# Expert rows past 128: gathered as quarter rows, turned by two 128x128 transposes, their results turned four chunks at a time

## The reference, cut to what matters

```
def moe(h, w_router, b_router, w_gate_up, b_gate_up, w_down, b_down):
    ...
    def expert_block(args):
        xb, e = args
        gu = xb @ w_gate_up[e] + b_gate_up[e]
        gate, up = gu[:, :D_EXPERT], gu[:, D_EXPERT:]
        gate = jnp.minimum(gate, SWIGLU_LIMIT)
        up = jnp.clip(up, -SWIGLU_LIMIT, SWIGLU_LIMIT)
        act = (up + 1.0) * gate * jax.nn.sigmoid(SWIGLU_ALPHA * gate)
        return act @ w_down[e] + b_down[e]
    ...
    y = y * gate_buf[:, None].astype(y.dtype)
    out = jnp.zeros((T + 1, D), y.dtype).at[tok_buf].add(y)[:T]
```

## Time and profile before

| | |
|---|---|
| median of 3 runs | 2743.37 us (2742.76 to 2745.33) |
| the profiled execution: its time | 2737.53 us |
| the profiled execution: span from first to last instruction | 2735.9 us |
| TensorE matmul busy | 2543.6 us, 93% of the span |
| VectorE, ScalarE, GpSimd busy | 850.0, 465.2, 274.2 us |
| mean granted clock of TensorE | 0.974 of full speed |
| experts stage, first to last transposed result | about 994 to 2551 us |

### The profile page before, as it was taken

The page is one execution under the profiler, slowest core; times in us unless marked ns, Lnnn a source line. Parts: engine busy times, 40 slices in busy tenths (PEclk is TensorE's granted clock), DMA queues, the critical chain, the costliest instruction groups (busy, mean ns, idle before and its releaser), DMA issues. The chain is left out here.

```text
span 2735.9 us, 46887 instructions
## 1 busy us (share of the span) xinstructions
PE 2543.6 (93%) x16462; PEld 2051.9 (75%) x16462; DVE 850.0 (31%) x2328; ACT 465.2 (17%) x1072; POOL 274.2 (10%) x421
## 2 busy tenths in 40 slices
PE   5897888999997949999999999999999999999599
PEld 3444665444444449999999999999999999999444
DVE  3425664000012342222222223232333333333353
ACT  3313442000000101111111111111111111111132
POOL 1420000000012210000000000000000000000220
PEclk9999999999998969999999999999999999999799
DMA  4000003011016467888888889899999999997441
GB/s 129 8 19 1 1 0 107 24 46 46 23 40 183 90 226 249 270 259 265 279 272 275 278 271 291 288 290 295 294 315 297 312 300 312 300 312 224 161 161 71
DMA packets 463940, 518.75 MB, mean 190 GB/s; under 512 B 16481, under 2 KB 440049, under 8 KB 463890
## 3 DMA queue, kind: packets, MB, share of 16 engines
q1 hardware_dynamic: 430898, 445.57, 52.4%
q0 software_dynamic: 14368, 38.95, 4.4%
q10 hardware_dynamic: 18624, 33.56, 3.6%
HBM read 484.33 MB, written 33.70 MB: 189 GB/s over the span
## 5 line engine op out<-in xcount | busy, mean ns | idle before, releaser
L1433 PE MATMUL bank<-arena_a,arena_w 128*128 128x128 f32 (+4 forms) x8192 | 977.4, 281 | 2.9 <-DVE bank L1525 2.9
L1433 PEld LDWEIGHTS bank<-arena_a,arena_w 128*128 128x128 f32 x8192 | 971.0, 191 | 3.2 <-issue 3.2
L1451 PE MATMUL bank<-arena_a,arena_w 128*128 128x128 f32 (+4 forms) x4096 | 517.0, 282 | 6.7 <-issue 6.7
L1451 PEld LDWEIGHTS bank<-arena_a,arena_w 128*128 128x128 f32 x4096 | 497.1, 191 | 12.9 <-issue 12.9
L1544 DVE TENSOR_SCALAR arena_m<-bank,arena_m 128x160 f32<-128x160 f32 x256 | 98.3, 384 | 631.1 <-PE bank L1433 631.1
L941 PE MATMUL bank<-arena_h,arena_w 128*128 128x512 f32 x512 | 224.4, 596 | 8.6 <-DMA arena_w<-in_w_pool_out_dram 8.6
L1555 DVE TENSOR_SCALAR arena_m<-bank,arena_m 128x160 f32<-128x160 f32 x256 | 98.3, 384 | 394.7 <-PE bank L1451 389.6
L941 PEld LDWEIGHTS bank<-arena_h,arena_w 128*128 128x128 f32 x512 | 98.0, 192 | 132.0 <-issue 123.2
L1496 ACT ACTIVATE arena_m<-arena_m 128x160 f32<-128x160 f32 x256 | 84.1, 336 | 662.1 <-DVE arena_m L1544 660.9
L1347 POOL DMA_DIRECT2D arena_m<-slot_tokens x33 | 19.4, 589 | 1227.7 <-issue 1225.2
L1502 ACT ACTIVATE arena_a<-bank 128x512 f32<-128x512 f32 x64 | 38.2, 597 | 612.1 <-PE bank L1465 612.1
(11 more groups left out here) (277 smaller groups left out, 2029.7 us busy)
## 6 DMA issues: line engine op xcount, KB each, us to landing
arena_w<-in_w_gate_up_dram SPq DMA_DIRECT2D x248, 1024.0 KB, 6.7
arena_w<-in_w_down_dram SPq DMA_DIRECT2D x124, 1024.0 KB, 6.6
expert_rows<-arena_a ACTq DMA_DIRECT2D x32, 512.0 KB, 2.8
arena_a<-in_x_dram SPq DMA_DIRECT2D x16, 512.0 KB, 4.2
arena_w<-in_w_in_dram SPq DMA_DIRECT2D x16, 512.0 KB, 5.2
arena_w<-in_w_gate_up_dram ACTq DMA_DIRECT2D x8, 1024.0 KB, 14.9
arena_w<-in_w_o_dram SPq DMA_DIRECT2D x1, 4096.0 KB, 16.0
x_rows<-arena_a SPq DMA_DIRECT2D x8, 512.0 KB, 6.7
```

The costliest lines, as they stand in the source:

```text
L1433: m = pe.matmul(GU[f % 3][:, to:to + width], w[c][:, k, at:at + P], xT[:, k, 0:width], start=(k == 0), stop=(k == K - 1), skip_group_check ...
L1451: m = pe.matmul(DN[d % 2][:, 0:width], wd[c][:, k, at:at + P], actT[:, k, 0:width], start=(k == 0), stop=(k == KF - 1))
```

## The change

**Gather.** The 32 rest rows are gathered as 128 quarter rows of 256 channels: row number r and quarter q together sit in partition 32q + r. GpSimd reads the 32 row numbers four times, into four partition groups, computes 4 x number + q in one instruction (with `quarter`, a column of 0, 1, 2, 3 that VectorE fills in the route stage) and gathers 128 pieces of 1 KB into `xq`. **Turning in.** Two 128x128 transposes of `xq` into `DN[0]` (now `x_rest`) replace the eight small ones; the eight main chunks go to `TX` and `DN[1]` (`x_bank`), four to a bank, and `GU[2]` is no longer used. ScalarE empties `TX` in one copy; VectorE empties `x_rest` in one strided copy and `DN[1]` in another. `down`'s first two steps now wait for VectorE's copies. **Turning back.** VectorE's bias add writes main and rest columns apart (`yT`, `yR`, all eight chunks kept), and the rest columns of four chunks are turned by one 128x128 transpose, behind chunks 3 and 7. ScalarE empties both halves of `YB` in one copy and stores them by two DMAs. **Start.** The zeroing of the banks is gone; `yR` and `yT` are zeroed in SBUF.

```diff
+                        for q in range(QUARTERS):
+                            dve.memset(quarter[q * REST:(q + 1) * REST, :], float(q)).then_inc(sem("quarter"), 1)
...
-        xg2 = view(arena_a, D, D)[0:REST, :]
+        QUARTERS = P // REST
+        QW = D // QUARTERS
+        xq = view(arena_a, D, QW)
...
-            pool.dma_start(idx_b, list_dram[bass.ds(slot + P, REST), :]).then_inc(rows_listed, 16)
-            wait_value(pool, rows_listed, 32 * i + 32)
+            for q in range(QUARTERS):
+                pool.dma_start(idx_b[q * REST:(q + 1) * REST, :], list_dram[bass.ds(slot + P, REST), :]).then_inc(rows_listed, 16)
+            wait_value(pool, rows_listed, 80 * i + 80)
+            pool.tensor_scalar(idx_q, idx_b, float(QUARTERS), quarter[:, :], ALU.mult, ALU.add).then_inc(rows_split, 1)
             pool.indirect_dma_start(xg, None, h2_dram, bass.IndirectOffsetOnAxis(idx_a, 0)).then_inc(rows_here, 16)
-            pool.indirect_dma_start(xg2, None, h2_dram, bass.IndirectOffsetOnAxis(idx_b, 0)).then_inc(rows_here, 16)
+            wait_value(pool, rows_split, i + 1)
+            pool.indirect_dma_start(xq, None, h2_quarters, bass.IndirectOffsetOnAxis(idx_q, 0)).then_inc(rows_here, 16)
...
                 GU, TX, DN, YA, YB = banks[0:3], banks[3], banks[4:6], banks[6], banks[7]
-                fill_bank = (DN[0], TX, DN[1], GU[2])
+                x_rest, x_bank = DN[0], (TX, DN[1])
...
                         def turn_x(i, rest):
                             wait_value(pe, rows_here, 32 * i + 32)
                             if rest:
-                                for j, bank in enumerate(fill_bank):
-                                    if j == 3 and not isinstance(i, int):
-                                        wait_value(pe, sem("gu_read"), KF * i - 2)
-                                    for h in (0, 1):
-                                        d = 2 * j + h
-                                        pe.transpose(bank[:, h * WIDTH + P:(h + 1) * WIDTH], xg2[:, d * P:(d + 1) * P], ident[0:REST, 0:REST])
-                            for j, bank in enumerate(fill_bank):
-                                if j == 3 and not rest:
-                                    wait_value(pe, sem("gu_read"), KF * i - 2)
                                 for h in (0, 1):
-                                    d = 2 * j + h
-                                    m = pe.transpose(bank[:, h * WIDTH:h * WIDTH + P], xg[:, d * P:(d + 1) * P], ident[:, :])
+                                    pe.transpose(x_rest[:, h * P:(h + 1) * P], xq[:, h * P:(h + 1) * P], ident[:, :])
+                            for j, bank in enumerate(x_bank):
+                                for h in range(4):
+                                    d = 4 * j + h
+                                    m = pe.transpose(bank[:, h * P:(h + 1) * P], xg[:, d * P:(d + 1) * P], ident[:, :])
                                 m.then_inc(sem("x_psum"), 1)
...
-                            wait_value(pe, sem("xT_act"), 2 * i + 2)
+                            wait_value(pe, sem("xT_act"), i + 1)
                             wait_value(pe, sem("xT_dve"), 2 * i + 2)
...
                                 if d < 2:
-                                    wait_value(pe, sem("xT_act"), 2 * i + (3 + d))
+                                    wait_value(pe, sem("xT_dve"), 2 * i + (3 + d))
...
                                 m.then_inc(sem("dn_psum"), 1)
+                                if d == 1:
+                                    wait_value(pe, sem("y_kept"), 3 * i + 3)
                                 if d == 5:
-                                    wait_value(pe, sem("y_kept"), 4 * i + 2)
+                                    wait_value(pe, sem("y_kept"), 3 * i + 4)
...
-                            if rest:
-                                pe.transpose(YB[0:REST, at], yT[d % 2][:, P:WIDTH], ident[:, :])
-                            pe.transpose(YA[:, at], yT[d % 2][:, 0:P], ident[:, :]).then_inc(sem("y_psum"), 1)
+                            if rest and d % 4 == 3:
+                                h = d // 4
+                                pe.transpose(YB[:, h * P:(h + 1) * P], yR[:, 4 * h:4 * h + 4, :].rearrange("p k t -> p (k t)"), ident[:, :])
+                            pe.transpose(YA[:, at], yT[:, d, :], ident[:, :]).then_inc(sem("y_psum"), 1)
...
-                        pe.wait_ge(sem("psum_set"), 4)
                         turn_x(0, True)
-                        pe.wait_ge(sem("psum_set"), 7)
...
                         def keep_x(i):
-                            for j in (0, 2):
-                                wait_value(act, sem("x_psum"), 4 * i + (j + 1))
-                                act.activation(xT[:, 2 * j:2 * j + 2, :].rearrange("p k t -> p (k t)"), fill_bank[j][:, 0:2 * WIDTH],
-                                               ACT.Copy).then_inc(sem("xT_act"), 1)
+                            wait_value(act, sem("x_psum"), 2 * i + 1)
+                            act.activation(xT[:, 0:4, 0:P], TX[:, :].rearrange("p (k t) -> p k t", t=P), ACT.Copy).then_inc(sem("xT_act"), 1)
...
                                 act.activation(y_a[:, at], YA[:, :], ACT.Copy).then_inc(sem("y_kept"), 1)
-                                act.activation(y_b[:, at], YB[0:REST, :], ACT.Copy).then_inc(sem("y_kept"), 1)
+                            act.activation(y_b.rearrange("p h c -> p (h c)"), YB[:, 0:2 * P], ACT.Copy).then_inc(sem("y_kept"), 1)
...
-                            act.dma_start(y_dram[bass.ds(row + P, REST), :], y_b).then_inc(sem("stored"), 16)
-                        wait_value(act, sem("stored"), 32 * n + 32)
+                            for h in (0, 1):
+                                to = y_dram[bass.ds(row + P, REST), h * BANK:(h + 1) * BANK]
+                                act.dma_start(to.rearrange("r (j c) -> j r c", c=P), y_b[:, h, :]).then_inc(sem("stored"), 16)
...
-                        for bank in fill_bank:
-                            dve.memset(bank[:, :], 0.0).then_inc(sem("psum_set"), 1)
-
                         def keep_x(i):
-                            for j in (1, 3):
-                                wait_value(dve, sem("x_psum"), 4 * i + (j + 1))
-                                dve.tensor_copy(xT[:, 2 * j:2 * j + 2, :].rearrange("p k t -> p (k t)"), fill_bank[j][:, 0:2 * WIDTH]
-                                                ).then_inc(sem("xT_dve"), 1)
+                            wait_value(dve, sem("x_psum"), 2 * i + 1)
+                            dve.tensor_copy(xT[:, :, P:WIDTH].rearrange("p (j h) r -> p h j r", h=2),
+                                            x_rest[:, 0:2 * P].rearrange("p (h j r) -> p h j r", h=2, r=REST)).then_inc(sem("xT_dve"), 1)
+                            wait_value(dve, sem("x_psum"), 2 * i + 2)
+                            dve.tensor_copy(xT[:, 4:8, 0:P], x_bank[1][:, :].rearrange("p (k t) -> p k t", t=P)).then_inc(sem("xT_dve"), 1)
...
-                        for bank in (GU[0], GU[1], YB):
-                            dve.memset(bank[:, :], 0.0).then_inc(sem("psum_set"), 1)
-                        dve.memset(yT[1], 0.0).then_inc(sem("yT"), 1)
+                        dve.memset(yR[:, :, :], 0.0)
+                        dve.memset(yT[:, :, :], 0.0).then_inc(sem("yT"), 1)
...
-                                if d >= 2:
-                                    wait_value(dve, sem("y_psum"), K * i + d)
-                                dve.tensor_scalar(yT[d % 2], DN[d % 2][:, 0:WIDTH], bias[:, 2 * KF + d:2 * KF + d + 1], None, ALU.add
+                                if d == 0:
+                                    wait_value(dve, sem("y_psum"), K * i + 1)
+                                dve.tensor_scalar(yR[:, d, :], DN[d % 2][:, P:WIDTH], bias[:, 2 * KF + d:2 * KF + d + 1], None, ALU.add)
+                                dve.tensor_scalar(yT[:, d, :], DN[d % 2][:, 0:P], bias[:, 2 * KF + d:2 * KF + d + 1], None, ALU.add
                                                   ).then_inc(sem("yT"), 1)
```

More of the change, by code:

```diff
@@ L158, in build @@
         iota_e = sb("iota_e", [P, E])
+        quarter = sb("quarter", [P, 1])
         dest_all = sb("dest_all", [P, T, TOP_K], I32)
@@ L1115, in _ @@
                         pool.wait_ge(sem("stored"), 32 * T)
+                        pool.wait_ge(sem("quarter"), QUARTERS)
                         gather_rows(pool, 0, 0)
@@ L1357, in experts @@
                 y_a = view(arena_a, 2 * D, D)
-                y_b = view(arena_a, 3 * D, D)[0:REST, :]
+                y_b = view(arena_a, 3 * D, 2, P)
                 xT = view(arena_a, 4 * D, K, WIDTH)
                 actT = view(arena_a, 4 * D + K * WIDTH, KF, WIDTH)
-                gc, sg, gs, yT = ([view(arena_m, WIDTH * (2 * j + b), WIDTH) for b in (0, 1)] for j in range(4))
+                gc, sg, gs = ([view(arena_m, WIDTH * (2 * j + b), WIDTH) for b in (0, 1)] for j in range(3))
```

(8 more changed lines are left out.)

12 lines of the change are left out of this document (8 added, 4 removed).

## The result

The changed kernel takes 2767.86 us (median of 4 runs, 2766.23 to 2768.90) against 2743.07 us (4 runs, 2741.27 to 2745.33): a ratio of 1.0095, 95% interval 1.0083 to 1.0107, or 24.8 us slower. The forecast was 2764, with a range of 2754 to 2778. The profiled execution took 2766.23 us, 28.7 us more than the one of before.

The account below looks back on a forecast made before the run. TensorE, busy 93% of the span, was taken as the bound; 5.4 (wide items) + 16.8 (narrow) - 2.6 (start) + 0.3 (gather) + 1.0 (end) = +20.9 us, on 2743.4 giving 2764.3 us; range 2754 to 2778.

Parts of the forecast that it names:

- The bound and the new wait: TensorE bounds the experts stage; `down` now waits in every item for VectorE's first copy, behind the last `swiglu`.
- Its size: `down` starts at G + 2.60 in wide items, 0.92 us later, and G + 2.69 in narrow ones, 1.18 later.
- Items together: Experts loop: 18 wide items lose 5.4 us in all, 14 narrow ones 16.8 us.
- The turn back: Wide items, after `down`'s products: six of eight rest transposes go, saving 0.62 us per item.
- The start: Start of the experts stage: first product 2.6 us earlier; the longer gather costs +0.3, covered by VectorE's last work.
- Start and gather together: Start of the experts stage: -2.6 us for the earlier first product and +0.3 for the gather in the route stage.
- The end: End of the experts stage: one more ScalarE store issue and small-piece stores cost +1.0 us, ends 0 and +4.
- C: Rival for `down`'s start: the copy comes in time, TensorE isn't held, -25 us, 2719 us; chance 0.05.
- E: Rival on TensorE's clock: idling ahead of `down` lowers it, +85 us or more, 2830 us; chance 0.04.
- D: Rival: the wait exists but is cheap, copy near its lower bound, start worth 5 us, about 2747 us; chance 0.03.
- the bounds of +14 and +35: Limits on the whole sum, from the strided copy's price (-5.4 to +9.0 us over 32 items) plus start and end.

Follow-up runs that it names:

- the wait alone: Kernel before, with only the banks of turned rows reordered so VectorE empties those `down` writes first: 2781.07 us, ratio 1.0140.
- the five reads alone: Kernel before, with the rest rows' numbers read three times more and one unused column computed, same rows gathered: 2744.68 us, ratio 1.0010.
- the last one: Changed kernel with turned rows in banks nobody waits for, and the first item's four rest-number reads issued by SyncE, not GpSimd: 2710.21 us, ratio 0.9886.

## Why the prediction was right, point by point

**The bound and the new wait: shown.** `down` is held by VectorE's first copy in all 32 items. Moving the copy's engine, its place in VectorE's order, and the banks each changes the wait as the chain says, and the wait alone, put into the kernel before, costs 38 us. That the 0.48 us gap of the earlier trace rows, called "issue", is the wait for ScalarE's copy was read rightly too: it goes when no copy is waited for.

**Its size: right to 0.02 us.** `down` starts at G + 2.71 in the wide item and in the narrow one; forecast 2.60 and 2.69. The copy took 0.416 us (forecast 0.41) and the product followed 0.10 us later (forecast 0.09). The other 0.09 us of the wide item are a shift of G itself, the start of the first transpose: VectorE's read of `gate_up`'s last bank begins 0.18 us behind G in the earlier trace rows (1091.15) and 0.27 behind it in the changed kernel (1097.12), since the new first transpose follows `gate_up`'s last product 0.13 us later and the old one 0.22. Counted from that read, `down` starts 2.44 us later in place of 1.50: the delay is 0.94 us for a forecast of 0.92, and 1.20 for 1.18 in the narrow item. The idle time in wide items came out as 1.45 us, outside the forecast 1.0 to 1.2: besides the 0.11 us, ten transposes at a pace of 0.11 us are through at G + 1.26, sooner than the 1.4 to 1.6 us that the forecast implied. It costs nothing; TensorE waits longer for the same copy. So "some 43 us" of idle time became 49.6.

**Items together: right.** Forecast 5.4 + 16.8; the traces have 5.3 us over 18 wide intervals from `down` to `down` (0.28 in the width of 152: 53.21 to 53.50) and 15.5 over 13 narrow ones (1.195 each: 45.45 to 46.64), forecast 0.3 and 1.2. Both terms of the wide item are right one by one: 0.94 us lost (forecast 0.92), 0.65 saved in the turn back (forecast 0.62).

**The turn back: shown.** The pace of 0.11 us held for 32 columns of weights and for 128. The Trainium skill ("TensorE: Matmul & The Clock Gate", section "LDWEIGHTS (loading the stationary operand)") says that a weight load costs by its columns, by which the turn back would save nothing. The trace does not agree in this place: with six loads of 32 columns fewer and two others widened to 128, the stage is 11.7 us shorter.

**The start: a term was mis-sized.** "VectorE's last work of the stage ends at 989.58 and is the cover; I take +0.3": the stretch ahead of the first transpose grew by 3.06 us, 2.06 of them with the five reads alone. The forecast had the gather land 6.6 us after its issue and nothing behind it. It landed 3.7 us after its issue in the kernel before, and a term that the forecast had at nothing stood behind it: GpSimd's drain, 3.00 us, which ended the stage already, by 0.36 us. So all that the new gather adds counts. Side by side, the two traces have 0.8 us more of wait for the last scatter ahead of the list reads (3.27 for 2.46), 1.8 more from the first list read to the issue of the second gather (forecast 1.9), 0.2 more until it has landed, 0.3 more of drain, and 0.1 less behind it. The first part is not the change's for certain: the kernel with the wait alone, which has the gather of before, waited 3.0 us there and has a stretch of 24.3 us. The first product after the first transpose came 2.3 us earlier (forecast 2.6). Start and gather together were forecast as -2.3 us and are +0.8 in the traces; that is most of the 3.6 us by which 2764.3 fell short of the median.

**The end: right.** +0.9 for a forecast of +1.0, up to TensorE's first instruction of the last stage; the first load of that stage is issued 1.5 us later than before, counted from the last `down`. The changed kernel's timeline, as in the earlier trace rows:

```profile
2579.16 0.38 ACT L1510 ACTIVATE arena_a<-bank 128x256 f32<-128x256 f32 x1
2579.77 0.36 ACTq L1514 DMA_DIRECT2D expert_rows<-arena_a  x1
2580.31 1.89 ACTq L1517 DMA_DIRECT2D expert_rows<-arena_a  x2
2584.92 0.35 SPq L1589 DMA_DIRECT2D arena_w<-x_rows  x1
```

The prediction had these stores on 4 of 16 DMA engines and no row for it. The trace of the changed kernel shows it, in the view of its DMA traffic from 2579 to 2586 us (busy share of the 16 engines in 40 slices, and the packets):

```profile
DMA  0000000008999999922122222222200000000009
...
DMA packets 416, 0.69 MB, mean 98 GB/s; under 512 B 24, under 2 KB 280, under 8 KB 416
```

The same view of before, from 2551.5 to 2556.5 us:

```profile
DMA  0000000000000999989999994990000000000000
...
DMA packets 192, 0.66 MB, mean 131 GB/s; under 512 B 32, under 2 KB 32, under 8 KB 192
```

While the store of 128 rows moves, the engines are nine tenths busy, and while the two new ones move, two tenths, which is what 4 of 16 make. The packets under 512 B, of 4 B each, go with the raising of the stores' semaphore: 24 for three stores where before has 32 for two. In the changed kernel the last two stores raise it four times each, 2583.48 to 2583.68 and 2584.31 to 2584.44.

**The rivals.** C, the faster one, had the right mechanism for another kernel: with the copy not waited for, it comes to 2710 and not to C's 2719. The narrow items gave 6.9 us (C: 6.4), but the wide ones 25.3 and not 17.1, since their ten transposes bring `down` forward by 0.68 us and not by 0.33. E is out: granted clock 1.00 from 1009 to 2583 us in the changed kernel, with 32 gaps of 1.45 to 1.67 us in it. Two sums of the prediction don't come out as written. D's terms don't reach its 2747 us: 20.9 less 5.4 for the copy, and the start worth 5 us in place of 2.6, is +13 us or 2756, and 2755 with gather and end at nothing. And the bounds of +14 and +35 give 2757 and 2778 us, not 2756 and 2776. Neither touches the forecast.

## What to carry to other kernels

When work is rearranged over PSUM banks, ask for each bank who must empty it before the next writer, and what stands ahead of that instruction in its engine's order: here six transposes fewer, and fewer banks, were worth -32 us or +21 us in the stage by which banks held the turned rows and who emptied them. A bank that is written late, or by nobody next, makes the same copy free. An engine's last compute instruction need not be the end of its stage: where GpSimd has issued gathers, look at its drain behind them, which took about 3 us here and was what the next stage waited for. SyncE's drain, behind its own DMAs in the same place, took 0.01 us.

## What was not expected of the hardware

- GpSimd's drain behind its last gather begins 0.19 us after the gather has landed and takes 3.00 us in the kernel before and in the one with the wait alone, 3.25 in the changed one and in five others, and 2.93 in the last one. It ended the route stage in all nine.
- ScalarE's queue was taken 1.89 us by the two stores of 512 B pieces in a four-part pattern (1.08 and 0.56 us, with a gap), against 0.34 for the one of 32 rows of 4 KB in the earlier trace rows. They ran on 4 of 16 DMA engines.
- The issue of the second, quarter-row gather took 1.79 us at the end of the route stage in the changed kernel, while the first took 1.06; with the lists read by SyncE it took 0.95. The five list reads ahead of a gather of 32 whole rows left its issue at 0.88 us (0.89 in the kernel before), so the list reads alone don't lengthen it. More isn't known; it was not tried by itself.
